# A mixture-of-experts layer in float32: the expert stage in quarter chunks, with its lists of tokens on chip

## The chip, the cores and the metric

The kernel runs on one core of a Trainium2 chip. A core has five engines that run side by side: TensorE (PE in the profile, with its weight loads as PEld), VectorE (DVE), ScalarE (ACT), GpSimd (POOL) and SyncE (SP), which here only issues DMAs. Engines wait for each other by semaphores. The metric is the time of one execution in microseconds, and less is better.

## What is computed

One decoder layer for 2048 tokens of width 1024: a mixer (gated linear attention and retention), and then a layer of 32 experts, each with a gate and up projection (1024 to 2048) and a down projection (1024 to 1024). Every token goes to its 4 best experts. The change concerns this second part:

```python
gu = lax.ragged_dot(xs, w_gu, group_sizes) + b_gu[sorted_e]
gate, up = jnp.split(gu, 2, axis=-1)
gate = jnp.minimum(gate, SWIGLU_LIMIT)
up = jnp.clip(up, -SWIGLU_LIMIT, SWIGLU_LIMIT)
act = (up + 1.0) * (gate * jax.nn.sigmoid(SWIGLU_ALPHA * gate))
out = lax.ragged_dot(act.astype(h.dtype), w_down, group_sizes) + b_down[sorted_e]
```

Run on the reference's inputs, the router gives 79 tiles of up to 128 tokens to the 32 experts: 3 2 1 1 4 3 1 4 3 1 2 1 4 1 2 2 2 3 1 1 2 2 5 2 3 1 5 2 8 2 1 4, in the order of the experts.

## The kernel before

Six phases run one after the other, with a barrier between them: modulation, projection, mixer, routing (`phase_routing`), experts (`phase_experts`) and the final norm.

At its end the routing phase works out a table of groups: an expert's tiles are cut into groups of up to four (`GT = 4`), so that its weights are loaded once for a group. The two experts with 5 tiles become 4 and 1, the one with 8 becomes 4 and 4: 35 groups for 32 experts, 47 places for them in the loops. Each engine runs the same loop over the groups and reads the table for itself (`field`, L1511: one load of a register from memory for each field). For places that hold no group it reads the number of tiles, finds 0 and goes on.

Within a group the weights come in six chunks of 1024 x 512 (`NCH`): four for gate and up (`NGU`), each of 256 gate and 256 up columns, and two for down. A chunk comes in two halves of 1 MB. Each half is loaded by SyncE in two DMAs with rows of 1 KB (L1568), rounded to a high part by ScalarE (`weights_hi`, L1634) and the rest is taken as a low part by VectorE (`weights_lo`, L1700). Four raw halves are held. A float32 product is then three products in the faster format: high by high, high by low, low by high (L111 to L113), so a tile takes 24 products of 128x512 for a chunk and 144 for its group. Two chunks of split weights are held, so ScalarE can write a half of chunk c + 2 once the last tile has gone past that half of chunk c.

Of a gate and up chunk VectorE adds the bias (L1716), clips (L1720, L1721), and multiplies (L1727, L1729) after ScalarE's sigmoid (L1674). Two transposes turn each result (`activations`, L1811), and it is split again (L1658, L1746). Of a down chunk VectorE multiplies by the token's share and g2 (`weigh`, L1755), and GpSimd adds the rows to `y_rows` in memory with an indirect DMA (L1617), which takes the rows' numbers from `rec_now`.

For the next group GpSimd loads the tokens' numbers (`rec_next`, L1581), gathers their rows (L1586), waits until they are there, and TensorE transposes them during the down chunks (`next_rows`, L1828). GpSimd does this after the last group's rows have landed in `y_rows` and after `rec_now` has come (L1605). ScalarE's first sigmoid of a group waits for the same landing (`y_added`), since `act_row` was a source of the last rows.

## Time and profile before

| | us |
|---|---|
| median of 3 runs (4604.93 to 4610.49) | 4606.93 |
| the profiled execution | 4608.54 |
| its span, first to last instruction | 4606.9 |
| of it, first to last product of the experts | 1546.1 to 4527.3 |

Twelve groups have one tile, ten two, five three and eight four. The profile's page lists the busy time of the engines, their groups of instructions and DMAs. The trace answers further questions: a timeline of single instructions (start, duration, and in brackets how long the engine had been idle and what ended that), busy times in chosen stretches, and groups of instructions by line. Times are from the start of the span.

### The profile page before, as it was taken

The page shows a single profiled execution, that of the slowest core. Times are in us where ns is not written, and L with a number is a line of the kernel's source. Part 1 is how long each engine was busy: PE and PEld are TensorE (multiplying, and loading weights), DVE is VectorE, ACT ScalarE, POOL GpSimd, SP SyncE. Part 2 cuts the span into 40 slices and gives each one's busy share as a digit, 9 for nine tenths or more (in the row PEclk, how much of TensorE's full clock was granted, in tenths as well). Part 3 has the DMA queues.
Part 4 walks back from the last instruction along what each step waited for, and adds up shares of the span by engine and source line. Part 5 has one row for each costly group of instructions (what it writes and reads, how often), then busy time and mean ns, then how long its engine had stood idle before and what let it go on. Part 6 is the DMA issues. An engine that isn't in the chain of part 4 may idle for free. (4 is left out here: it accounts for less than half of the span.)

```text
span 4606.9 us, 64078 instructions
## 1 busy us (share of the span) xinstructions
PE 4043.3 (88%) x18375; PEld 3256.1 (71%) x18376; DVE 2660.6 (58%) x4097; ACT 1566.9 (34%) x2223; POOL 779.6 (17%) x691
## 2 busy tenths in 40 slices
PE   7998996665898697998999999998999999999993
PEld 4886885554676575887877777876877777788772
DVE  4123123997566567556567667667657665655752
ACT  2213112555121234224244334444324333322422
POOL 1010011554122111011112011111111111110101
PEclk8998997787998799999999999999999999999996
DMA  6342333332221568356468477667648557644735
GB/s 230 110 163 97 110 132 117 107 108 102 104 105 73 165 193 275 120 148 209 133 191 250 144 223 228 200 205 256 208 117 265 164 182 203 203 126 116 236 96 168
DMA packets 557045, 758.35 MB, mean 165 GB/s; under 512 B 32602, under 2 KB 462980, under 8 KB 552372
## 3 DMA queue, kind: packets, MB, share of 16 engines
q1 hardware_dynamic: 494532, 587.16, 38.8%
q0 software_dynamic: 59856, 160.36, 13.4%
q10 hardware_dynamic: 2592, 9.96, 0.5%
q8 instruction: 40, 0.66, 0.1%
q14 instruction: 25, 0.20, 0.0%
HBM read 649.31 MB, written 108.07 MB: 164 GB/s over the span
## 5 line engine op out<-in xcount | busy, mean ns | idle before, releaser
L1700 DVE TENSOR_TENSOR exp_w_lo<-exp_w_raw,exp_w_hi 128x2048 fp32r<-128x2048 f32 x420 | 959.3, 2288 | 273.5 <-ACT exp_w_hi L1634 145.8
L111 PE MATMUL exp_bank_acc<-exp_w_hi,exp_x_hi 128*128 128x512 f32 x2528 | 1022.5, 404 | 87.4 <-DVE exp_w_lo L1700 65.9
L113 PE MATMUL exp_bank_acc<-exp_w_hi,exp_x_lo 128*128 128x512 f32 x2528 | 996.1, 394 | 0.0
L112 PE MATMUL exp_bank_acc<-exp_w_lo,exp_x_hi 128*128 128x512 f32 x2528 | 994.5, 393 | 0.0
L1634 ACT CAST exp_w_hi<-exp_w_raw 128x2048 fp32r<-128x2048 f32 x420 | 788.9, 1910 | 318.4 <-PE exp_bank_acc L113 255.1
L111 PEld LDWEIGHTS exp_bank_acc<-exp_w_hi,exp_x_hi 128*128 128x128 f32 x2528 | 480.5, 190 | 218.2 <-issue 85.3
L111 PE MATMUL exp_bank_acc<-exp_w_hi,exp_a_hi 128*128 128x512 f32 x1264 | 511.5, 405 | 61.2 <-DVE exp_a_lo L1746 43.5
L113 PEld LDWEIGHTS exp_bank_acc<-exp_w_hi,exp_x_lo 128*128 128x128 f32 x2528 | 480.0, 190 | 103.9
L112 PEld LDWEIGHTS exp_bank_acc<-exp_w_lo,exp_x_hi 128*128 128x128 f32 x2528 | 481.6, 191 | 92.4
L113 PE MATMUL exp_bank_acc<-exp_w_hi,exp_a_lo 128*128 128x512 f32 x1264 | 494.9, 392 | 0.0
L112 PE MATMUL exp_bank_acc<-exp_w_lo,exp_a_hi 128*128 128x512 f32 x1264 | 493.8, 391 | 0.0
L1617 POOL DMA_INDIRECT y_rows<-exp_weighted,exp_rec_now x100 | 162.8, 1628 | 1714.0 <-DVE exp_weighted L1755 1624.2
L1674 ACT ACTIVATE exp_act_row<-exp_gate_up 128x256 f32<-128x256 f32 x316 | 132.1, 418 | 799.4 <-DVE exp_gate_up L1720 694.2
L111 PE MATMUL pro_bank_acc<-pro_w_hi,pro_h_hi 128*128 128x512 f32 x896 | 356.1, 397 | 0.0
L113 PE MATMUL pro_bank_acc<-pro_w_hi,pro_h_lo 128*128 128x512 f32 x896 | 351.1, 392 | 0.0
L112 PE MATMUL pro_bank_acc<-pro_w_lo,pro_h_hi 128*128 128x512 f32 x896 | 351.0, 392 | 0.0
L1658 ACT CAST exp_a_hi<-exp_bank_ta 128x256 fp32r<-128x256 f32 x316 | 116.8, 370 | 625.5 <-PE exp_bank_ta L1811 625.5
L111 PEld LDWEIGHTS exp_bank_acc<-exp_w_hi,exp_a_hi 128*128 128x128 f32 x1264 | 238.1, 188 | 122.2 <-DVE exp_a_lo L1746 50.6
L1746 DVE TENSOR_TENSOR exp_a_lo<-exp_bank_ta,exp_a_hi 128x256 fp32r<-128x256 f32 x316 | 133.5, 422 | 278.0 <-ACT exp_a_hi L1658 263.6
L113 PEld LDWEIGHTS exp_bank_acc<-exp_w_hi,exp_a_lo 128*128 128x128 f32 x1264 | 237.7, 188 | 51.2
L112 PEld LDWEIGHTS exp_bank_acc<-exp_w_lo,exp_a_hi 128*128 128x128 f32 x1264 | 238.6, 189 | 43.7
L1716 DVE TENSOR_TENSOR exp_gate_up<-exp_bank_acc,exp_bias 128x512 f32<-128x512 f32 x316 | 215.8, 683 | 92.4 <-PE exp_bank_acc L113 90.9
(292 smaller groups left out, 4898.1 us busy)
## 6 DMA issues: line engine op xcount, KB each, us to landing
exp_w_raw<-in_w_gu SPq DMA_DIRECT2D x560, 512.0 KB
exp_w_raw<-in_w_down SPq DMA_DIRECT2D x280, 512.0 KB
exp_bias<-in_b_gu SPq DMA_DIRECT2D x35, 1024.0 KB, 8.4
early_w_raw<-in_w_in POOLq DMA_DIRECT2D x14, 2048.0 KB, 10.9
proj<-pro_stage SPq DMA_DIRECT2D x112, 256.0 KB
pro_w_ada<-in_w_ada POOLq DMA_DIRECT2D x64, 256.0 KB, 3.6
mix_proj<-proj SPq DMA_DIRECT2D x16, 768.0 KB, 4.6
mod_w_ada<-in_w_ada SPq DMA_DIRECT2D x8, 1024.0 KB, 15.1
```

The lines of the kernel that those rows point to most:

```text
L111: nc.tensor.matmul(out, act_hi, w_hi, start=first, stop=False)
L112: nc.tensor.matmul(out, act_hi, w_lo, start=False, stop=False)
L113: return nc.tensor.matmul(out, act_lo, w_hi, start=False, stop=last)
L1617: pool.indirect_dma_start(out=keep["y"][c - NGU], out_offset=bass.IndirectOffsetOnAxis(ap=rec_now[:, t, 0:1], axis=0), in_=weighted_at(c, ...
L1634: nc.scalar.copy(whi[:, c % 2, half * HK:(half + 1) * HK], raw[:, n % RAW]).then_inc(hi_done, 1)
L1658: nc.scalar.copy(ahi[:, t, 2 * c:2 * c + 2], ta[:]).then_inc(ahi_done, 1)
L1674: nc.scalar.activation(act_row[:, t], gu[:, t % 2, 0:H], ACT.Sigmoid, scale=SIG).then_inc(sg_done, 1)
L1700: nc.vector.tensor_tensor(wlo[:, c % 2, rows], raw[:, n % RAW], whi[:, c % 2, rows], ALU.subtract).then_inc(lo_done, 1)
L1716: nc.vector.tensor_tensor(gu[:, u].rearrange("p (a n) -> p a n", a=2), acc[:, bank(c, t)].rearrange("p (a n) -> p a n", a=2), bias[:, :, c ...
L1746: nc.vector.tensor_tensor(alo[:, t, 2 * c:2 * c + 2], ta[:], ahi[:, t, 2 * c:2 * c + 2], ALU.subtract).then_inc(alo_done, 1)
```

## The change

All of it is in the experts' phase, but for the table.

1. Weights in quarters: a chunk's 8 row blocks are loaded, rounded, subtracted and multiplied in 4 pieces of 512 KB (`PIECES = 4`), one DMA each with rows of 2 KB. Eight raw pieces are held, as many bytes as before. TensorE waits for each piece by itself in the first tile, and releases each by itself.
2. A chunk of gate and up is now 512 columns of gate (chunks 0 and 2) or of up (chunks 1 and 3). Bias, gate and product are done on 512 columns once per pair: one addition and one Silu for the gate; addition, clip and product for up. Four transposes per pair replace two per chunk. ScalarE now casts half of chunk 2 ahead of the gates of all tiles, and half of chunk 4 ahead of the second pair's gates.
3. Records on chip: all tokens' numbers and shares are loaded once (`rec`, 512 KB), and GpSimd copies a group's numbers with two small instructions. `rec_next`, `rec_now` and their waits are gone. The gather for the next group is issued ahead of all waits for landings, and its own landing isn't waited for on GpSimd.
4. Each landing is waited for by the instruction that overwrites the source. The last result of tile 0 goes through `gu[:, 1]`, all others through `act_row`.
5. Packed fields: tiles, next tiles, tiles before and place come in one word, with shifts. A count of groups replaces the reading of empty places.
6. Even last groups: where an expert's last group would have one tile, it takes one from the group before (5 tiles: 3 and 2).

```diff
             fin(nc.vector.tensor_scalar(table[:, 1:2], col[:, 6:7], float(GT), 0.0, ALU.min, ALU.max))
+
+            one = sel[:, 0:1]
+            fin(nc.vector.tensor_scalar(one, col[:, 6:7], 1.0, None, ALU.is_equal))
+            fin(nc.vector.scalar_tensor_tensor(out=one, in0=col[:, 5:6], scalar=0.0, in1=one, op0=ALU.is_gt, op1=ALU.mult))
+            fin(nc.vector.scalar_tensor_tensor(out=table[:, 1:2], in0=col[:, 6:7], scalar=GT + 1.0, in1=table[:, 1:2],
+                                               op0=ALU.is_equal, op1=ALU.subtract))
+            fin(nc.vector.tensor_tensor(table[:, 1:2], one, table[:, 1:2], ALU.subtract))
+            fin(nc.vector.tensor_tensor(col[:, 5:6], col[:, 5:6], one, ALU.subtract))
...
+    NCH, NGU = 6, 4
+    PIECES = 4
+    SK = KD // PIECES
+    RAW = 2 * PIECES
+    raw = k.sb("w_raw", [P, RAW, SK, N])
...
+    def place_in(w):
+        return (w >> 14).with_bounds(min_val=0, max_val=PLACES - GT)
...
-        def __init__(self, eng, g, T):
-            self.T = T
-            self.before = field(eng, g, BEFORE, NG * GT)
+        def __init__(self, eng, g):
+            self.word = load_word(eng, g)
+            self.T = tiles_in(self.word)
+            self.nT = (self.word >> 3) & 7
+            self.before = (self.word >> 6) & 255
...
                     expert = field(sp, g, EXPERT, E - 1)
-                    for n in range(2 * NCH):
-                        c, half = n // 2, n % 2
+                    for n in range(PIECES * NCH):
+                        c, j = n // PIECES, n % PIECES
                         if n == RAW:
 
-                            sp.wait_ge(act_done, G.before * NGU + 1)
-                            sp.dma_start(bias[:].rearrange("p a n -> p (a n)"),
-                                         gu_b[bass.ds(expert, 1), :].rearrange("o n -> (o n)").partition_broadcast(P)
+                            sp.wait_ge(act_done, G.before * 2 + 1)
+                            sp.dma_start(bias[:], gu_b[bass.ds(expert, 1), :].rearrange("o n -> (o n)").partition_broadcast(P)
                                          ).then_inc(bias_in, 16)
...
+                        sp.wait_ge(lo_done, G.pieces(n - RAW + 1))
+                        rows = slice(j * SK, (j + 1) * SK)
+                        w, col = (gu_w, column(c)) if c < NGU else (dn_w, (c - NGU) * N)
+                        sp.dma_start(raw[:, n % RAW], w[:, bass.ds(expert, 1), rows, col:col + N]).then_inc(raw_in[n % RAW], 16)
...
+            pool.wait_ge(rec_in, 16)
+            pool.sem_inc(wait_carrier, 1)
+            pool.wait_ge(word_set, 1)
+            for half in range(2):
+                pool.dma_start(keep["y"][half][S:S + 1, 0:NG + 1].bitcast(I32), word[:]).then_inc(y_out[half], 16)
+
+            def fetch_rows(g, T, place):
+
+                nc.gpsimd.tensor_copy(next_token[:], rec[:, bass.ds(place, GT), 0]).then_inc(next_set, 1)
+                pool.wait_ge(next_set, g + 1)
                 pool.sem_inc(wait_carrier, 1)
                 for t in range(GT):
...
-                pool.wait_ge(rows_in, (before + T) * 16)
-                pool.sem_inc(wait_carrier, 1)
...
-                    with pool.If(nT > 0):
+                with pool.If(count > g):
+                    G = Group(pool, g)
+                    place, nplace = place_in(G.word), place_in(load_word(pool, g + 1))
+                    with pool.If(G.nT > 0):
                         pool.wait_ge(tx_done, G.before + G.T + 1)
                         pool.sem_inc(wait_carrier, 1)
-                        fetch_rows(g + 1, nT, nplace, nbefore)
+                        fetch_rows(g + 1, G.nT, nplace)
+                    for half in range(2):
+                        pool.wait_ge(y_out[half], G.landed(0))
+                        pool.sem_inc(wait_carrier, 1)
+                    nc.gpsimd.tensor_copy(token[:], rec[:, bass.ds(place, GT), 0]).then_inc(token_set, 1)
+                    nc.gpsimd.tensor_copy(share[:], rec[:].bitcast(F32)[:, bass.ds(place, GT), 1]).then_inc(share_set, 1)
+                    pool.wait_ge(token_set, g + 1)
+                    pool.sem_inc(wait_carrier, 1)
                     for c in (NGU, NGU + 1):
                         for t in range(GT):
                             with pool.If(G.T > t):
-                                pool.wait_ge(weighted_done, G.down_tile(c, t))
+                                pool.wait_ge(read_done, G.chunk_tile(c, t))
                                 pool.sem_inc(wait_carrier, 1)
                                 pool.indirect_dma_start(
                                     out=keep["y"][c - NGU],
...
+                                    out_offset=bass.IndirectOffsetOnAxis(ap=token[:, t:t + 1], axis=0),
+                                    in_=weighted_at(c, t), in_offset=None, compute_op=ALU.add).then_inc(y_out[c - NGU], 16)
+            for half in range(2):
+                pool.wait_ge(y_out[half], total * 16 + 16)
...
             def weights_hi(g, n, freed):
 
...
+                act.wait_ge(raw_in[n % RAW], (g * (PIECES * NCH // RAW) + n // RAW + 1) * 16)
+                c, j = n // PIECES, n % PIECES
+                act.wait_ge(mm_piece[j], freed)
+                nc.scalar.copy(whi[:, c % 2, j * SK:(j + 1) * SK], raw[:, n % RAW]).then_inc(hi_done, 1)
 
...
+                    def gate(q, t):
+
+                        act.wait_ge(read_done, G.chunk_tile(2 * q, t))
+                        nc.scalar.activation(act_row[:, t], gu[:, t % 2], ACT.Silu, scale=SIG).then_inc(sg_done, 1)
 
                     def next_rows_hi(t):
                         with act.If(nT > t):
                             rows_hi(G.before + G.T, t)
 
...
+                    for n in range(PIECES, 2 * PIECES + PIECES // 2):
+                        weights_hi(g, n, G.chunks_before(n // PIECES - 1))
+                    for t in range(GT):
+                        with act.If(G.T > t):
+                            if t < 2:
+
+                                act.wait_ge(y_out[t], G.landed(0))
+                            gate(0, t)
+                    for n in range(2 * PIECES + PIECES // 2, 4 * PIECES):
+                        weights_hi(g, n, G.chunks_before(n // PIECES - 1))
+                    for t in range(GT):
+                        with act.If(G.T > t):
+                            activations_hi(0, t)
+                    for n in range(4 * PIECES, 4 * PIECES + PIECES // 2):
+                        weights_hi(g, n, G.chunks_before(3))
+                    for t in range(GT):
+                        with act.If(G.T > t):
+                            gate(1, t)
+                    for n in range(4 * PIECES + PIECES // 2, 5 * PIECES + PIECES // 2):
+                        weights_hi(g, n, G.chunks_before(n // PIECES - 1))
+                    activations_hi(1, 0)
                     next_rows_hi(0)
-                    weights_hi(g, 2 * NCH - 1, G.chunks_before(NGU))
+                    for n in range(5 * PIECES + PIECES // 2, 6 * PIECES):
+                        weights_hi(g, n, G.chunks_before(NGU))
                     for t in range(1, GT):
                         with act.If(G.T > t):
-                            activations_hi(NGU - 1, t)
+                            activations_hi(1, t)
...
+            def gate_bias(G, g, q, t):
+
+                c = 2 * q
+                if q == 0 and t == 0:
                     dve.wait_ge(bias_in, (g + 1) * 16)
-                u = t % 2
-                dve.wait_ge(act_done, G.gu_tile(c, t) - 1)
+                if q == 0 and t == 1:
+                    dve.wait_ge(y_out[1], G.landed(0))
+                if q == 0 and t < 2:
+                    dve.wait_ge(act_done, G.before * 2 + 1)
+                elif t < 2:
+                    dve.wait_ge(act_done, G.before * 2 + G.T + 1)
+                else:
+                    dve.wait_ge(sg_done, G.pair_tile(q, t - 2) - 1)
                 dve.wait_ge(mm_done, G.chunk_tile(c, t))
-                nc.vector.tensor_tensor(gu[:, u].rearrange("p (a n) -> p a n", a=2),
-                                        acc[:, bank(c, t)].rearrange("p (a n) -> p a n", a=2),
-                                        bias[:, :, c * H:(c + 1) * H], ALU.add).then_inc(read_done, 1)
+                nc.vector.tensor_tensor(gu[:, t % 2], acc[:, bank(c, t)], bias[:, column(c):column(c) + N],
+                                        ALU.add).then_inc(read_done, 1)
+
+            def up_times_gate(G, q, t):
+
+                c, u = 2 * q + 1, t % 2
+                dve.wait_ge(mm_done, G.chunk_tile(c, t))
+                if t < 2:
+                    dve.wait_ge(sg_done, G.before * 2 + G.T * (q + 1))
+                else:
+                    dve.wait_ge(act_done, G.pair_tile(q, t - 2))
+                nc.vector.scalar_tensor_tensor(out=gu[:, u], in0=acc[:, bank(c, t)], scalar=1.0,
+                                               in1=bias[:, column(c):column(c) + N], op0=ALU.add,
+                                               op1=ALU.add).then_inc(read_done, 1)
                 dve.wait_ge(read_done, G.chunk_tile(c, t))
...
+                nc.vector.tensor_scalar(gu[:, u], gu[:, u], LIMIT + 1.0, 1.0 - LIMIT, ALU.min, ALU.max).then_inc(clip_step, 1)
+                dve.wait_ge(clip_step, G.pair_tile(q, t) - 1)
+                nc.vector.scalar_tensor_tensor(out=act_row[:, t], in0=act_row[:, t], scalar=float(MOST_GATE),
+                                               in1=gu[:, u], op0=ALU.min, op1=ALU.mult).then_inc(act_done, 1)
...
+                        if c == NGU and t == 0:
+                            dve.wait_ge(share_set, G.g + 1)
+                        if c == NGU + 1 and t == 0:
+                            dve.wait_ge(y_out[1], G.landed(0))
+                        if c == NGU + 1 and t == 1:
+                            dve.wait_ge(y_out[0], G.landed(G.T))
...
+                        for n in range(PIECES):
+                            weights_lo(g, PIECES * (c + 1) + n)
                         for t in range(GT):
                             with dve.If(G.T > t):
...
+                                if c == 2:
+                                    activations_lo(0, t)
+                                if c % 2 == 0:
+                                    gate_bias(G, g, c // 2, t)
+                                else:
+                                    up_times_gate(G, c // 2, t)
+                    activations_lo(1, 0)
+                    for n in range(5 * PIECES, 5 * PIECES + PIECES // 2):
+                        weights_lo(g, n)
                     next_rows_lo(0)
-                    weights_lo(g, 2 * NCH - 1)
-                    dve.wait_ge(rec_now_in, (g + 1) * 16)
-                    dve.sem_inc(wait_carrier, 1)
+                    for n in range(5 * PIECES + PIECES // 2, 6 * PIECES):
+                        weights_lo(g, n)
...
-                                    if s == HK:
-                                        mm.then_inc(mm_half, 1)
+                                    if s and s % SK == 0:
+                                        mm.then_inc(mm_piece[s // SK - 1], 1)
                                         if t == 0:
-                                            pe.wait_ge(lo_done, G.halves(2 * c + 2))
+                                            pe.wait_ge(lo_done, G.pieces(PIECES * c + s // SK + 1))
+                                    if c == 2 and s == KD - 2:
+                                        activations(G, 0, t)
+                                    if c == NGU - 1 and t == 1 and s == KD // 2:
+                                        activations(G, 1, 0)
                                     if c == NGU and t > 0 and s == 0:
...
+                                        activations(G, 1, t)
+                                    if c == NGU and t == 0:
+                                        if s == 0:
+                                            pe.wait_ge(alo_done, G.before * 2 + G.T + 1)
+                                        if s == KD // 2:
                                             with pe.If(G.T < 2):
-                                                activations(G, NGU - 1, t)
+                                                activations(G, 1, t)
                                             next_rows(0)
-                                        pe.wait_ge(alo_done, G.gu_tile(NGU - 1, t))
+                                    if c == NGU and s == KD // 2:
+                                        pe.wait_ge(alo_done, G.pair_tile(1, t))
```

## Rows read from the trace of the kernel before

**Rows 1.** the page: busy us of each engine, share of the span, instructions

```profile
PE 4043.3 (88%) x18375; PEld 3256.1 (71%) x18376; DVE 2660.6 (58%) x4097; ACT 1566.9 (34%) x2223; POOL 779.6 (17%) x691
```

**Rows 2.** stretches: three of ten one-tile groups; the sum is of all ten

```profile
1770.70:1834.60 63.90, 45.41 (x184) 35.05 (x184) 43.43 (x46) 27.59 (x27) 12.28 (x8) 0.89 0.87 275
...
2378.70:2424.70 46.00, 38.22 (x169) 29.11 (x169) 37.95 (x42) 27.28 (x24) 7.18 (x6) 1.00 0.84 263
2498.60:2551.20 52.60, 40.89 (x185) 30.50 (x185) 41.68 (x45) 27.61 (x27) 13.24 (x9) 1.00 0.95 291
...
sum 511.50, PE 400.85 PEld 301.52 DVE 399.95 ACT 272.80 POOL 98.20; mean PE 40.09 PEld 30.15 DVE 39.99 ACT 27.28 POOL 9.82
```

**Rows 3.** stretches: one expert's groups of four and one tile; three tiles; two tiles

```profile
3307.20:3445.00 137.80, 136.07 (x616) 111.69 (x616) 72.26 (x120) 38.19 (x50) 16.84 (x11) 1.00 0.44 121
3445.00:3490.90 45.90, 38.24 (x168) 29.08 (x168) 38.11 (x42) 27.39 (x25) 8.24 (x6) 1.00 0.85 262
...
2274.50:2378.70 104.20, 102.46 (x464) 83.97 (x464) 60.55 (x93) 32.43 (x39) 11.60 (x9) 1.00 0.53 151
3490.90:3563.40 72.50, 70.58 (x328) 57.90 (x329) 54.03 (x72) 31.52 (x35) 10.45 (x9) 1.00 0.82 257
```

**Rows 4.** timeline of VectorE over one chunk of a one-tile group

```profile
2389.61 2.29 DVE L1700 TENSOR_TENSOR exp_w_lo<-exp_w_raw,exp_w_hi 128x2048 fp32r<-128x2048 f32 x1 [0.28 <-issue]
...
2392.62 0.68 DVE L1716 TENSOR_TENSOR exp_gate_up<-exp_bank_acc,exp_bias 128x512 f32<-128x512 f32 x1
...
2393.74 2.29 DVE L1700 TENSOR_TENSOR exp_w_lo<-exp_w_raw,exp_w_hi 128x2048 fp32r<-128x2048 f32 x1
...
2397.09 2.29 DVE L1700 TENSOR_TENSOR exp_w_lo<-exp_w_raw,exp_w_hi 128x2048 fp32r<-128x2048 f32 x1 [0.27 <-issue]
```

**Rows 5.** timeline of VectorE: where that group begins; two subtractions in a row

```profile
2382.91 2.29 DVE L1700 TENSOR_TENSOR exp_w_lo<-exp_w_raw,exp_w_hi 128x2048 fp32r<-128x2048 f32 x1 [3.54 <-issue]
...
2422.08 4.48 DVE L1700 TENSOR_TENSOR exp_w_lo<-exp_w_raw,exp_w_hi 128x2048 fp32r<-128x2048 f32 x2
```

**Rows 6.** timeline of TensorE: after transposes; five products in a row; two stalls

```profile
1570.42 0.48 PE L111 MATMUL exp_bank_acc<-exp_w_hi,exp_x_hi 128*128 128x512 f32 x1
1570.74 0.40 PE L112 MATMUL exp_bank_acc<-exp_w_lo,exp_x_hi 128*128 128x512 f32 x1
...
2382.95 0.39 PE L111 MATMUL exp_bank_acc<-exp_w_hi,exp_x_hi 128*128 128x512 f32 x1
...
2384.08 0.39 PE L113 MATMUL exp_bank_acc<-exp_w_hi,exp_x_lo 128*128 128x512 f32 x1
...
2346.54 1.04 PE L1803 MATMUL exp_bank_tx<-keep_const,exp_rows 128*128 128x128 f32 x8
2349.12 0.50 PE L111 MATMUL exp_bank_acc<-exp_w_hi,exp_a_hi 128*128 128x512 f32 x1 [1.54 <-DVE exp_a_lo L1746]
...
2396.09 0.50 PE L111 MATMUL exp_bank_acc<-exp_w_hi,exp_x_hi 128*128 128x512 f32 x1 [0.93 <-DVE exp_w_lo L1700]
```

**Rows 7.** groups of instructions: busy us, mean ns | idle before, releaser

```profile
L1700 DVE TENSOR_TENSOR exp_w_lo<-exp_w_raw,exp_w_hi 128x2048 fp32r<-128x2048 f32 x420 | 959.3, 2288 | 273.5 <-ACT exp_w_hi L1634 145.8 <-issue 118.8 <-DVE exp_weighted L1755 8.2
...
L1755 DVE SCALAR_TENSOR_TENSOR exp_weighted<-exp_bank_acc,exp_rec_now,exp_g 128x512 f32<-128x512 f32 x100 | 74.9, 749 | 245.9 <-PE exp_bank_acc L113 245.9
...
L1328 DVE TENSOR_TENSOR rou_h<-rou_h,rou_sh 128x1024 f32<-128x1024 f32 x16 | 19.6, 1225 | 0.6
...
L404 ACT ACTIVATE pro_squares<-early_x 128x1024 bf16<-128x1024 f32 x16 | 17.0, 1060 | 5.7 <-DMA early_x<-in_x 5.6
```

**Rows 8.** instructions of single lines: table loads, last accumulation, GpSimd's loop (min/median/max ns)

```profile
L1512 POOLq TENSOR_LOAD <-exp_table x223: 282/287/501, 1518.7 to 4547.1; - x112
...
L1617 POOL DMA_INDIRECT y_rows<-exp_weighted,exp_rec_now x100: 1541/1562/3575, 1628.7 to 4529.0; - x100
...
L1595 POOLq COMPARE_BRANCH  x47: 40/45/53, 1660.1 to 4547.9; - x47
```

**Rows 9.** a stretch in which SyncE loads rows of 2 KB (w_ada)

```profile
3.00:20.00 17.00, 10.88 (x20) 4.80 (x21) 4.41 (x13) 0.00 (x0) 0.80 (x2) 1.00 1.03 384
```

270 lines of the change are left out of this document (109 added, 161 removed).

## Prediction

> **What bounds it now.** The page first: TensorE is busy for 88% of the span, VectorE for 58% [rows 1]. Those are averages, and the chain of waits at the page's end only follows the final norm, so I read the stretches group by group. In groups of two, three and four tiles TensorE is busy all but 2 us (70.58 of 72.5, 102.46 of 104.2, 136.07 of 137.8) [rows 3]. In the ten one-tile groups of [rows 2] (the two that follow a group of four of their own expert are set apart) it is busy for 400.85 of 511.5 us. One, of 46.0 us, is typical; with four tiles next it is 52.6; the worst, right behind another one-tile group, takes 63.9. So TensorE bounds the large groups and something else the small ones. The instruction counts give the followers: 144 products and 8 transposes, and 8 for each next tile (160, 168 or 184; two, three and five of the ten).
>
> The timeline of VectorE shows what. Over one chunk of a one-tile group it goes from one subtraction (2389.61) to the same one of the next chunk (2397.09), 7.48 us, with next to no gap [rows 4]: 2 x 2.20 for weights (two in a row last 4.48, so the second starts 2.19 after the first [rows 5]), the rest for bias, clip, products and a split. TensorE needs 24 products for it. Five take 2384.08 - 2382.95 = 1.13 us, so one takes 0.226 and a chunk 5.44. It waits for `exp_w_lo`, here 0.93 us by the trace and 1.3 us from start to start, since an earlier product's tail is counted as busy [rows 6].
>
> **One-tile groups, the term that carries the sum.** VectorE's work per group. Weights: before, 12 subtractions at 2.20 from start to start. A 128x1024 one lasts 1.225 where 128x2048 lasts 2.288 [rows 7]. Back to back they overlap by 0.09, so 24 cost 24 x 1.135 = 27.2 against 26.4: 0.8 us more. The rest of four chunks was 4 x (7.48 - 4.40) = 12.3. Now it is two pairs, each gate bias 0.70, up (addition 0.77, clip about 0.45, product 0.77) 2.0, and split 0.65, some 3.35 and 0.5 for registers: 7.7. At the group's start VectorE stands for 3.54 us while it reads its fields [rows 5]. One load instead of three leaves 1.5 to 2: I take 1.7. Together: 0.8 - 4.6 - 1.8 = -5.6 us.
>
> The Trainium skill speaks against the quarters. VectorE: DVE Perf Modes, section on the TRN2 errata, has a fixed cost for each instruction on SBUF, (N+151)/0.96 ns, and advises large tiles. Its 1.224 us is the trace's 1.225; without the overlap that the trace shows, 24 would cost 2.1 us more than I take, 21 us over ten groups.
>
> What the end of a group depends on is TensorE, so I lay the new order out by hand, from its first product at 0, for two tiles next. VectorE subtracts pieces 4 to 7 by 6.9 (chunk 1 starts at 5.44 and wants a piece every 1.36: no stall), adds the gate bias by 7.6, pieces 8 to 11 by 12.3, up by 14.4. TensorE turns that at 15.0, inside chunk 2. Pieces 12 to 15 by 19.1, split and second gate 20.6, pieces 16 to 19 by 25.3, up 27.4. Here is the one long stall: TensorE has come to the middle of chunk 4 at 24.9 and waits until 27.5, turns it, turns next rows (8 transposes in 1.04 at most [rows 6]; I take 0.9), waits 0.6 for the split, and goes on at 29.5. Chunk 5 runs from 32.2 to 38.6. So 38.6 for two tiles next, 37.6 for one, 39.7 for three and 42.1 for four, where VectorE's split of rows comes between. ScalarE at 1.06 us for each piece [rows 7] stays ahead. A hand schedule leaves out waits: I take 39.5, 40.5, 42 and 44.5. Behind a one-tile group VectorE is late by some 3 us, and the bias comes late too (its DMA goes out after piece 7 of the next group rather than half 3): 48 and 45 for the two such. The ten: 2 x 39.5 + 2 x 40.5 + 45 + 3 x 44.5 + 42 (its follower has now three tiles) + 48 = 428.5. **Gain 83.** The bare schedule gives 406 (105). The floor is TensorE's busy 400.85.
>
> The waits of GpSimd go: it no longer loads records, and issues the gather some 20 us earlier. ScalarE's first gate waits only for the landing of half 0, issued a whole chunk before. The 63.9 us group holds most of this: 16 of the 83.
>
> **Even last groups.** Two experts with 5 tiles. Before, 137.8 + 45.9 = 183.7; now a group of three and one of two, 104.2 + 72.5 = 176.7 as they are [rows 3], 174.5 with the edits below. **Gain 2 x 9.2 = 18.4.**
>
> **Two tiles and more.** Removed: the stall in the middle of chunk 4, where TensorE waited for the split of tile 0 (1.54 shown, about 1.7 from start to start) [rows 6], since that result is now turned in chunk 3. The first product after transposes starts 0.32 before the next rather than 0.23 [rows 6]: 0.09, twice less per tile. Fewer loads at the group's edge, 0.3. Added, with no row that shows it: ScalarE holds all gates of the second pair until it has cast pieces 16 and 17, which need the last tile of chunk 2. `gu` has two buffers, so the gate bias of tile 2 waits for the gate of tile 0. Queued behind it on VectorE are pieces 16 to 19 and the up of tile 0, which TensorE wants at 8.2 us into chunk 3. By hand that comes at 7.6 for two tiles, 9.4 for three, 10.8 for four: no stall, 1.3 and 2.7. In chunk 4 the split of tile 1 stands behind pieces 20 to 23: 0 to 0.8, I take 0.75. Per group: 1.7 for two tiles (ten), 0.5 for three (five), -0.8 for four (six). **Gain 15.** The added waits are 44 us in all (12 x 0.75 + 7 x 2.05 + 6 x 3.45, with the groups of the edit above), so the bounds are 59 without them and -29 with twice as much.
>
> **Edges.** Last accumulation issued at 4529.0, GpSimd's loop ends at 4547.9 [rows 8]. Between lie its landing and 12 empty places, about 1.17 us each. One load (0.287) and its register work go from each: **gain 8**, 5 to 12. Start: `rec` (512 KB) before the first gather, the word, two small DMAs, in place of one record load: loss 2, bounds 0 to 8. Routing: seven small VectorE steps of 0.2: loss 1.4.
>
> **The sum**, on the profiled execution of 4608.5: 83 + 18.4 + 15 + 8 - 2 - 1.4 = 121, so 4487.5. The median stands 1.6 below that execution: **4486 us**, 2.6% less.
>
> **Rivals.** (a) *DMA takes VectorE's place.* For: in one-tile groups the DMA engines are busy 0.84 to 0.95 of the time [rows 2]. Against: they move 263 to 291 GB/s there in rows of 1 KB, about 310 for a full share, and 384 where SyncE loads rows of 2 KB [rows 9], as all weights now come. The ten groups' 140 MB (some 274 GB/s over 511.5 us) take 379 us at 370 GB/s, under 428, but 451 at 311. Were the larger rows worth nothing and the queues 0.95 full, they would take 475: 46 less gained, 4532.
>
> The Trainium skill, DMA: Bandwidth & Descriptors, section Bandwidth, advises DMAs of 1 MiB and more; these stay at 512 KB, and by the rule nothing would be gained from the larger rows. Rows 9 show 384 with DMAs of 1 MB.
>
> (b) *The gathered gates and waits cost more in large groups*, twice my estimate, since VectorE's order puts whatever is late ahead of pieces that others need: 44 less gained, 4530.
>
> (c) *Slower.* The same mechanism, stronger: ScalarE is in order, and stands at pieces 8 and 9 until the last tile of chunk 0, with all first gates behind it, and again at 16 and 17. If VectorE then falls behind by more than its slack, which is a chunk of one tile, 5.44 us, for each of the two pairs, every group of three or four (13 after the change) loses 2 x 5.4 us and more: 13 x 11 = 143 more than I take. That outweighs the 121 of gain: 4629. It decides from 9.3 us per group. Against: in a group of four VectorE is busy 72 of 138 us [rows 3], so it catches up.
>
> (d) *The schedule without my surcharge and without added waits*: 22 + 44 more, 4420.
>
> **Chances.** Forecast (4455 to 4515) 0.58; (a) 0.14; (b) 0.12; (d) 0.09; (c) 0.07. Range 4436 to 4550: it takes in (a) and (b) with some 20 us beyond, and leaves out (c) and the better half of (d). Under 0.2% is about what a measurement can't tell from no change. Faster by more: 0.92; within: 0.01; slower: 0.07.
>
> **What would show it.** Right: one-tile groups of 39 to 45 us, VectorE back to back in them, the worst near 48; `exp_rows` gathers in the first third of a group; the wait of TensorE for `exp_a_lo` gone in large groups and a wait for `exp_act_row` of 1 to 3 us in chunk 3 of those with three and four tiles; DMA share under 0.95 at over 300 GB/s; some 8 us less between the last product and the final norm. Wrong: ScalarE waiting for `exp_w_raw` in most one-tile groups (a), TensorE idle over 5 us in large groups (b, c), or one-tile groups still near 46.

## The result, and the profile after

The changed kernel takes 4440.72 us (median of 4 runs, 4436.95 to 4445.28), the kernel before 4608.71 us beside it. The ratio is 0.9636 (95% interval 0.9619 to 0.9653), and the time lies 45 us under the 4486 forecast. The profiled execution has a span of 4443.7 us where before it was 4606.9.

I split both spans at the first product of each group. All in us; the rows are rounded one by one:

| part of the span | before | after | gain | forecast |
|---|---|---|---|---|
| ten one-tile groups | 511.5 | 424.1 | 87.4 | 83 |
| two experts with five tiles | 369.8 | 347.9 | 21.9 | 18.4 |
| ten other groups of two | 730.7 | 698.5 | 32.2 | 17 |
| five other groups of three | 524.6 | 520.0 | 4.6 | 2.5 |
| six groups of four | 844.8 | 840.2 | 4.6 | -4.8 |
| ahead of the first product | 1546.1 | 1548.2 | -2.1 | -3.4 |
| behind the last product | 79.6 | 64.9 | 14.7 | 8 |
| span | 4606.9 | 4443.7 | 163.2 | 120.7 |

The busy times, from the page of the changed kernel (for [rows 1]):

```profile
PE 3998.1 (90%) x18375; PEld 3255.1 (73%) x18376; DVE 2431.6 (55%) x3422; ACT 1573.4 (35%) x2327; POOL 749.7 (17%) x728
```

TensorE issues the same 18375 instructions; that it is busy for 45 us less goes with the stalls, whose first part counts as the tail of the product ahead, and with some 12 us less at half clock (see the part on the clock below). VectorE lost 675 instructions and 229 us.

The one-tile groups of the changed kernel, to be held against [rows 2] (columns: stretch, its length, busy us of PE, PEld, DVE, ACT and POOL, granted clock, share of the DMA engines, GB/s):

```profile
1761.90:1811.50 49.60, 39.79 (x184) 30.48 (x184) 40.27 (x44) 28.65 (x35) 11.76 (x9) 1.00 1.00 353
...
2344.80:2383.10 38.30, 36.13 (x169) 29.18 (x167) 34.97 (x39) 27.70 (x32) 7.23 (x7) 1.00 0.92 308
2452.00:2498.20 46.20, 40.02 (x186) 32.01 (x184) 39.43 (x43) 27.73 (x34) 9.02 (x9) 0.96 0.96 323
...
sum 424.00, PE 378.56 PEld 302.05 DVE 371.20 ACT 276.11 POOL 78.68; mean PE 37.86 PEld 30.20 DVE 37.12 ACT 27.61 POOL 7.87
```

The typical one fell from 46.0 to 38.3, the one with four tiles next from 52.6 to 46.2, the worst from 63.9 to 49.6. The last has a full DMA share. The larger groups, for [rows 3]: an expert's three and two tiles, three tiles, two tiles behind a one-tile group, four tiles:

```profile
3210.40:3314.60 104.20, 103.18 (x474) 84.97 (x473) 52.74 (x64) 33.12 (x40) 12.96 (x12) 1.00 0.56 163
3314.60:3384.20 69.60, 69.28 (x321) 57.17 (x320) 45.13 (x52) 30.88 (x36) 8.83 (x9) 1.00 0.69 213
2241.50:2344.80 103.30, 102.28 (x466) 84.13 (x465) 51.56 (x62) 32.27 (x38) 11.08 (x10) 1.00 0.52 152
2383.10:2452.00 68.90, 68.54 (x312) 56.49 (x313) 46.01 (x52) 30.52 (x35) 11.62 (x8) 1.00 0.80 262
2498.20:2636.40 138.20, 135.96 (x617) 112.02 (x618) 59.77 (x76) 37.41 (x45) 15.09 (x12) 1.00 0.44 132
```

Groups of two are now TensorE and nothing else (68.54 of 68.9); in a group of four 2.2 us are still idle.

The best single view is TensorE's own waits over the experts' part (what for: us in total, times, longest). Before:

```profile
PE exp_bank_acc L111 <- DVE exp_w_lo L1700: 82.7, 98, 3.3
PE exp_bank_acc L111 <- DVE exp_a_lo L1746: 43.5, 29, 2.4
PE exp_bank_acc L111 <- issue: 19.3, 27, 2.5
PE exp_bank_tx L1803 <- DVE exp_x_lo L1706: 13.0, 11, 2.0
PE exp_bank_tx L1803 <- DMA exp_rows<-h_rows,exp_rec_next: 9.6, 6, 3.5
PE exp_bank_ta L1811 <- DVE exp_act_row L1729: 4.7, 3, 2.5
```

And after:

```profile
PE exp_bank_ta L1884 <- DVE exp_act_row L1797: 37.7, 25, 3.9
PE exp_bank_acc L112 <- DVE exp_w_lo L1757: 18.4, 16, 1.9
PE exp_bank_acc L112 <- DVE exp_a_lo L1815: 9.1, 32, 0.4
PE exp_bank_tx L1876 <- DVE exp_x_lo L1763: 6.9, 6, 2.0
PE exp_bank_acc L112 <- issue: 1.1, 2, 0.8
```

Register work and gathered rows are no longer waited for to speak of. The waits for the low parts of weights and activations (`exp_w_lo`, `exp_a_lo`) fell from 126.2 us to 27.5. One wait grew from 4.7 to 37.7, that for the activations before they are turned (`exp_act_row`).

### The profile page after: what moved, and what is told of

Same layout as the page of the kernel before. It is cut to its first block and busy times, and to the rows that moved or that the text cites. A ratio compares the mean times of both kernels' runs of the same rounds, so it can differ in the third digit from the quotient of the medians.

```text
span 4443.7 us, 64529 instructions
## 1 busy us (share of the span) xinstructions
PE 3998.1 (90%) x18375; PEld 3255.1 (73%) x18376; DVE 2431.6 (55%) x3422; ACT 1573.4 (35%) x2327; POOL 749.7 (17%) x728
## 5 line engine op out<-in xcount | busy, mean ns | idle before, releaser
L1664 ACT CAST exp_w_hi<-exp_w_raw 128x1024 fp32r<-128x1024 f32 x840 | 860.7, 1051 | 949.3 <-PE exp_bank_acc L114 834.5
L1757 DVE TENSOR_TENSOR exp_w_lo<-exp_w_raw,exp_w_hi 128x1024 fp32r<-128x1024 f32 x840 | 978.0, 1217 | 64.5 <-ACT exp_w_hi L1664 59.6
L112 PE MATMUL exp_bank_acc<-exp_w_hi,exp_x_hi 128*128 128x512 f32 x2528 | 999.8, 395 | 15.0 <-DVE exp_w_lo L1757 12.9
L1646 POOL DMA_INDIRECT y_rows<-exp_act_row,exp_token x123 | 195.6, 1590 | 2147.1 <-DVE exp_act_row L1827 2100.5
L1791 DVE SCALAR_TENSOR_TENSOR exp_gate_up<-exp_bank_acc,exp_bias 128x512 f32<-128x512 f32 x158 | 108.9, 689 | 320.4 <-PE exp_bank_acc L114 320.0
L1827 DVE SCALAR_TENSOR_TENSOR exp_act_row<-exp_bank_acc,exp_share,exp_g 128x512 f32<-128x512 f32 x123 | 92.0, 748 | 331.1 <-PE exp_bank_acc L114 322.7
L1780 DVE TENSOR_TENSOR exp_gate_up<-exp_bank_acc,exp_bias 128x512 f32<-128x512 f32 x158 | 108.4, 686 | 263.8 <-PE exp_bank_acc L114 117.3
L1688 ACT CAST exp_a_hi<-exp_bank_ta 128x512 fp32r<-128x512 f32 x158 | 92.4, 585 | 452.7 <-PE exp_bank_ta L1884 452.7
```

The lines of the kernel that those rows point to most:

```text
L112: nc.tensor.matmul(out, act_hi, w_hi, start=first, stop=False)
L1646: pool.indirect_dma_start(out=keep["y"][c - NGU], out_offset=bass.IndirectOffsetOnAxis(ap=token[:, t:t + 1], axis=0), in_=weighted_at(c, t ...
L1664: nc.scalar.copy(whi[:, c % 2, j * SK:(j + 1) * SK], raw[:, n % RAW]).then_inc(hi_done, 1)
L1688: nc.scalar.copy(ahi[:, t, 4 * q:4 * q + 4], ta[:]).then_inc(ahi_done, 1)
L1757: nc.vector.tensor_tensor(wlo[:, c % 2, rows], raw[:, n % RAW], whi[:, c % 2, rows], ALU.subtract).then_inc(lo_done, 1)
L1780: nc.vector.tensor_tensor(gu[:, t % 2], acc[:, bank(c, t)], bias[:, column(c):column(c) + N], ALU.add).then_inc(read_done, 1)
```

## The experiments

The theory of the prediction: VectorE's work and the order of its queue set the one-tile groups, TensorE the others, and the added waits cost a little in groups of three and four. The chief rival: DMA, either the weights' rate or the landings that GpSimd waits for. Unless it says otherwise, a run is the changed kernel with one edit. Each run was timed beside the kernel before on its chip (its medians there 4604.8 to 4607.5, here 4608.7), so two ratios differ surely where their intervals are apart. Durations of groups are cut as in the table above.

**1. The gate of the second pair, earlier.**

```diff
                         with act.If(G.T > t):
+                            if t > 0:
+                                gate(1, t - 1)
                             activations_hi(0, t)
...
                         with act.If(G.T > t):
-                            gate(1, t)
+                            with act.If(G.T < t + 2):
+                                gate(1, t)
```

> The changed kernel with one thing moved: ScalarE issues the second pair's gate of tile t - 1 between the casts of the first pair's activations of tiles t - 1 and t, and not after the casts of all tiles and half of chunk 4's weights; the gate of the last tile stays where it is. Theory of the queue order: the stalls of 1.1 us (three tiles) and 2.3 us (four tiles) in chunk 3, in which TensorE waits for the first pair's activations, come from a late gate, since the up products of tiles 0 and 1 free their accumulators only behind it. Then the stalls go in the 7 groups of three and the 6 groups of four tiles: 7 x 1.1 + 6 x 2.3 = 21.5 us at most, so about 4420 us, and one-tile groups stay within 0.5 us each. Rival: VectorE's own work sets those stalls, and the gates would have been on time. Then the large groups stay within 0.3 us each and the time is that of the changed kernel, 4441 us. Third: the early gates delay the casts of the activations, and the transposes of pair 0 wait for them: four-tile groups get longer by 1 us per cast behind a gate, 6 x 3 us, about 4459 us.

Measured: 4414.18 us, ratio 0.9585 (0.9572 to 0.9598), apart from the changed kernel's. Groups of three fell by 1.2 us each (728.5 to 720.0 for seven), groups of four by 3.1 (840.2 to 821.8 for six), one-tile groups by 4.1 in all, of which 2.7 in a single one (44.4 to 41.7). TensorE in a group of four, first the changed kernel and then this one (start, duration, idle before):

```profile
2573.45 0.39 PE L114 MATMUL exp_bank_acc<-exp_w_hi,exp_x_lo 128*128 128x512 f32 x1
2575.90 0.65 PE L1884 MATMUL exp_bank_ta<-keep_const,exp_act_row 128*128 128x128 f32 x4 [2.07 <-DVE exp_act_row L1797]
```

```profile
2559.08 0.40 PE L114 MATMUL exp_bank_acc<-exp_w_hi,exp_x_lo 128*128 128x512 f32 x1
2559.32 0.60 PE L1887 MATMUL exp_bank_ta<-keep_const,exp_act_row 128*128 128x128 f32 x4
```

The stall of 2.45 us from start to start is 0.24. The theory of the queue order holds, against VectorE's own work. In groups of four that is 2.2 of the 3.1 us; most of the rest is TensorE's granted clock, which in the changed kernel was at half for 22 products of these groups and here for none (see the part on the clock below). This version is faster than both kernels; of those that leave out no work only run 12 equals it.

**2. Without even last groups.**

```diff
-            one = sel[:, 0:1]
-            fin(nc.vector.tensor_scalar(one, col[:, 6:7], 1.0, None, ALU.is_equal))
...
-            fin(nc.vector.tensor_tensor(col[:, 5:6], col[:, 5:6], one, ALU.subtract))
```

> The changed kernel without the rule for even last groups: five tiles are again a group of four and a group of one. By the trace of the changed kernel a group of four tiles takes 139 to 140 us and one of one tile 43 us, two groups of three and two tiles 104.2 + 69.7 = 173.9 us. Theory of the sum (two experts, each 139.5 + 43 - 173.9 = 8.6 us): 17 us slower, about 4458 us. Rival: the group of one tile behind a large group finds its weights already there and costs only its TensorE work of 35 us, which the next group does not pay back: 0.6 us per expert, within 3 us of the changed kernel.

Measured: 4451.49 us, 0.9663 (0.9648 to 0.9678): 10.8 more by the medians, 6.7 by the spans, and the interval still touches that of the changed kernel. The groups say more: the two experts' pairs take 139.8 + 37.9 and 138.2 + 38.4 us where three and two tiles take 104.2 + 69.7 and 104.3 + 69.7, so 6.4 more in all, and the one-tile group ahead of one of them 45.6 rather than 41.1, since it has four tiles next. The result lies between my two cases and, by the intervals, is not surely apart from no change. A one-tile group behind a large one of its own expert costs 38, not the mean of 43 that I had put in.

**3. Halves of a chunk.**

```diff
-    PIECES = 4
+    PIECES = 2
```

> The changed kernel with PIECES = 2: each chunk comes in two pieces of 1 MB and no longer in four of 512 KB; everything else stays (rows of 2 KB, casts on 128x2048). Theory of the prediction: the size of the pieces sets how much of VectorE's and ScalarE's work lies ahead of the first product of a chunk that is late, since TensorE cannot begin with a piece before it is subtracted whole. One-tile groups: at each of 6 chunks the start comes later by one quarter, 1.1 us, as far as the chunk is late at all, which holds for 2 to 4 of the 6: 2 to 4 us for each of ten groups, 20 to 45 us in all, about 4475 us. Rival 1: the gain of the one-tile groups is VectorE's work that was taken away (fewer and larger instructions), and the pieces do nothing: within 10 us of the changed kernel, and rather faster, because half as many instructions save 0.1 us each where VectorE is bound. Rival 2: DMA sets the one-tile groups; pieces of twice the size are moved as fast, and each raw piece is freed later, so single groups behind one another get longer by 3 us or more each in the rows in which ScalarE waits for a raw piece. The Trainium skill (DMA: Bandwidth & Descriptors) asks for DMAs of 1 MiB and more; by it the larger pieces would come faster and these waits would shrink.

Measured: 4484.0 us, 0.9729 (0.9714 to 0.9744). One-tile groups +2.1 each (445.4 in all), two tiles +0.5, three +0.5, four +1.3. TensorE's waits:

```profile
PE exp_bank_acc L112 <- DVE exp_w_lo L1757: 42.3, 27, 4.2
PE exp_bank_ta L1884 <- DVE exp_act_row L1797: 29.5, 24, 3.2
PE exp_bank_acc L112 <- DVE exp_a_lo L1815: 18.7, 33, 0.6
```

`exp_w_lo` is at 42.3 where quarters have 18.4, and the split of the activations at 18.7 against 9.1. VectorE has half as many subtractions, and the kernel is slower, with TensorE waiting longer for the low parts: what counts is how much stands ahead of the first product. (The casts and the DMAs became larger too, so their shares are not told apart; and of the 8 us that the groups of four lost, some 3.6 are 18 more products at half clock.) By the Trainium skill (DMA: Bandwidth & Descriptors, section Bandwidth) the pieces of 1 MB would come faster; ScalarE waited 97.7 us for raw pieces here and 92.3 in the changed kernel, so no such gain shows.

**4. Rows of 1 KB.**

```diff
-                        sp.dma_start(raw[:, n % RAW], w[:, bass.ds(expert, 1), rows, col:col + N]).then_inc(raw_in[n % RAW], 16)
+                        for part in range(2):
+                            cols = slice(part * (N // 2), (part + 1) * (N // 2))
+                            sp.dma_start(raw[:, n % RAW, :, cols],
+                                         w[:, bass.ds(expert, 1), rows, col + cols.start:col + cols.stop]).then_inc(raw_in[n % RAW], 16)
```

> The changed kernel with each piece of weights loaded by two DMAs whose rows are 1 KB, as they were before the change, and not by one with rows of 2 KB; the bytes and their order stay. Theory of VectorE and queue order: large groups have cover, and the one-tile groups are bound by VectorE and TensorE, not by the loads: within 10 us of the changed kernel, 4441 to 4451 us. Rival, DMA sets the time of the one-tile groups (12.6 MB of weights in 38 to 50 us are 250 to 330 GB/s): the kernel before moved at most about 310 to 330 GB/s with rows of 1 KB, the changed one 370 to 384 GB/s. Then the ten one-tile groups get longer by 3 to 6 us each, 30 to 60 us in all, 4471 to 4501 us, and most in the groups behind another one-tile group.

(Each piece then comes as two DMAs of 256 KB; ScalarE's wait counts both.) Measured: 4446.66 us, 0.9654 (0.964 to 0.9669), not to be told from the changed kernel. The ten one-tile groups take 425.2 us. The DMA engines had a little more to do for the same bytes (in one such group a share of 0.97 at 299 GB/s, in the changed kernel 0.90 at 299), but the time did not follow. The larger rows, on which my case against rival (a) leaned, were worth next to nothing.

**5. The kernel before, with half of the subtractions.**

```diff
                 rows = slice(half * HK, (half + 1) * HK)
-                nc.vector.tensor_tensor(wlo[:, c % 2, rows], raw[:, n % RAW], whi[:, c % 2, rows],
+                rows = slice(half * HK, half * HK + HK // 2)
+                nc.vector.tensor_tensor(wlo[:, c % 2, rows], raw[:, n % RAW, 0:HK // 2], whi[:, c % 2, rows],
```

> The kernel before, in which VectorE subtracts only the first half of each half of the weights; the low part of the other half is left out (set to zero once ahead of the loop), while TensorE multiplies as before. A subtraction takes 1.22 us instead of 2.29, 12 per group: 13 us less of VectorE's work. Theory, VectorE's work sets the ten one-tile groups of the kernel before (VectorE busy for 399.95 of 511.5 us, TensorE for 400.85): they fall to 415 to 440 us in all, so some 80 us less than before, 4525 us, and the large groups move little. Rival, the waits for records and landings set them: the ten stay over 490 us, and the time is within 20 us of the kernel before. In between, what is left above 415 to 440 is the share of the waits and of DMA.

The other half of the low part is left out (zero), TensorE multiplies as before. Measured: 4537.48 us, 0.9849 (0.9833 to 0.9866), 70 less than the kernel before. But the ten one-tile groups fell only from 511.5 to 485.2, near the rival's 490; the rest came in the other groups, above all behind one-tile groups (two tiles: 73.9 to 70.1, 74.8 to 70.6). Why so little, TensorE's waits tell:

```profile
PE exp_bank_tx L1807 <- DMA exp_rows<-h_rows,exp_rec_next: 40.5, 9, 6.7
PE exp_bank_acc L111 <- DVE exp_w_lo L1704: 29.6, 47, 2.2
PE exp_bank_acc L111 <- DVE exp_a_lo L1750: 13.1, 23, 1.3
```

`exp_w_lo` fell from 82.7 to 29.6, and the gathered rows rose from 9.6 to 40.5. A second part is the clock: TensorE ran 75 products of the ten groups at half clock, where the kernel before ran 25, some 10 us of the missing gain. Still, the kernel before had two bounds in the same groups, one right behind the other: VectorE, and a gather whose first part was issued 20 to 32 us into the group. What made it late was above all the load of records. GpSimd's waits in the kernel before:

```profile
POOL exp_rec_next L1581 <- DMA exp_rec_now<-places: 137.3, 34, 5.5
POOL exp_rows L1586 <- DMA exp_rec_next<-places: 101.6, 33, 5.7
```

That is 7 us in each group. My theory named only the first bound.

**6. The changed kernel, with half of the subtractions.**

```diff
-                nc.vector.tensor_tensor(wlo[:, c % 2, rows], raw[:, n % RAW], whi[:, c % 2, rows],
+                rows = slice(j * SK, j * SK + SK // 2)
+                nc.vector.tensor_tensor(wlo[:, c % 2, rows], raw[:, n % RAW, 0:SK // 2], whi[:, c % 2, rows],
```

> The changed kernel with the same cut: VectorE subtracts only the first half of each piece, 128x512 in place of 128x1024, some 0.66 us in place of 1.22; the low part of the other half of the weights is left out (zero). 24 x 0.55 = 13 us less of VectorE's work per group. Theory, VectorE's work still sets the one-tile groups: they fall from 424 to some 375 to 390 us in all (TensorE is busy for 35 to 40 us in each), and the one right behind another falls from 49.6 and 44.4 to near 42; the time is 4441 - 40 = 4400 us, a little less with the stalls of large groups. Rival, DMA sets the groups that have four tiles next (41 to 50 us) and those behind another one-tile group: these six stay above 42 us, only the four at 38 lose 1 to 2 us each, and the time is within 12 us of 4441, in spite of a third less work on VectorE.

The same work is left out. Measured: 4386.42 us, 0.9525 (0.9509 to 0.9541). The ten fell from 424.1 to 398.2, where TensorE was busy for 378.6 in the changed kernel. Where one or two tiles come next they take 35.3 and 36.2, which is TensorE alone (but 42.0 behind another one-tile group). The four with four next keep 42.2 to 47.4, 2 to 4 us less than in the changed kernel, with VectorE busy for only 28:

```profile
2042.00:2084.90 42.90, 38.43 (x185) 30.86 (x183) 28.09 (x45) 27.54 (x34) 8.25 (x9) 1.00 0.94 334
1754.50:1802.00 47.50, 41.15 (x186) 32.98 (x185) 28.25 (x45) 28.62 (x35) 8.26 (x10) 0.93 1.04 375
```

So VectorE sets the groups at 38 us. In the six above 40 something else takes over after 2 to 4 us. The loads are the likely part of it, since ScalarE still waits there, but no run took them away, so this is argued and not shown; the turns and splits of up to four next tiles are in those groups as well. In the worst group of the changed kernel ScalarE waits for raw pieces (first line the total in that group, then single casts):

```profile
ACT exp_w_hi L1664 <- DMA exp_w_raw<-in_w_gu: 14.2, 8, 4.4
```

```profile
1764.86 1.05 ACT L1664 CAST exp_w_hi<-exp_w_raw 128x1024 fp32r<-128x1024 f32 x1 [1.95 <-DMA exp_w_raw<-in_w_gu]
1770.30 1.05 ACT L1664 CAST exp_w_hi<-exp_w_raw 128x1024 fp32r<-128x1024 f32 x1 [4.39 <-DMA exp_w_raw<-in_w_gu]
```

**7. A later gather, and 8. one as late as before.**

```diff
                         pool.wait_ge(tx_done, G.before + G.T + 1)
                         pool.sem_inc(wait_carrier, 1)
+                        pool.wait_ge(read_done, G.chunk_tile(2, 0))
+                        pool.sem_inc(wait_carrier, 1)
                         fetch_rows(g + 1, G.nT, nplace)
```

(This is run 8. Run 7 has these lines without the two new ones, but behind the waits for `y_out`, and a wait for `rows_in` behind them.)

> The changed kernel with the gather of the next group's rows issued where the kernel before issued it, behind GpSimd's wait for the landing of the group's previous results, and with its own landing waited for on GpSimd before the group's numbers are copied. Theory of the prediction: rows are wanted only in chunk 4, and the early gather does nothing for the time but in the group behind another one-tile group, within 5 us of 4441. Rival 1: the early gather carries part of the gain, since a late one delays the turns of the next rows: 2 to 4 us for each one-tile group, 20 to 40 us slower. Rival 2: the early gather is harmful, since its 512 KB per tile stand ahead of the weights of chunks 2 and 3 on the same engines, just where ScalarE waits for a raw piece (1.4 and 3.0 us in the one-tile group with four tiles next): then the late one is faster by 1 to 3 us in each of the six one-tile groups of over 40 us, 6 to 18 us in all.

> The changed kernel with the gather of the next group's rows issued as late as the kernel before issued it: GpSimd waits first until VectorE has added the gate bias of chunk 2 of tile 0, which is 21 us into a one-tile group (before: 20 to 31 us; changed kernel: 5 to 13; the run late_gather: 9 to 20, at no cost). Theory, the gather was a second bound right behind VectorE's work: in the kernel before with VectorE's subtractions halved, TensorE waited up to 3.5 us for the gathered rows in the middle of chunk 4. Rows are wanted some 27 us into the group and land 4.4 to 11.6 us behind their issue: with one tile next 0 to 1 us, with two 2 to 3, with three 4, with four 6 us for each group. 2 x 0.5 + 3 x 2.5 + 4 + 4 x 6 = 36 us, about 4477 us; large groups unchanged. Rival: VectorE alone sets one-tile groups and TensorE would have stood anyway at that place: within 8 us of 4441.

Measured, run 7: 4442.78 us, 0.9645 (0.9629 to 0.9661), no difference; the gathers went out 9 to 21 us into the one-tile groups, the first of each at 9 to 16. Run 8: 4486.16 us, 0.9736 (0.972 to 0.9752), 45.4 more. All of it is in the ten one-tile groups (424.1 to 469.3: +1.8 and 3.2 with one tile next, 1.6 to 4.8 with two, 5.4 with three, 3.6 to 7.8 with four); the groups of two stay within 0.1 us, those of three but for the first too, and those of four take 0.5 less on the mean. Some 5 of the 45 us are again the clock (41 products at half clock in the ten groups, not 15). TensorE's wait for the rows:

```profile
PE exp_bank_tx L1878 <- DMA exp_rows<-h_rows,exp_next_token: 63.5, 10, 10.4
```

Together the two runs draw the line: with its first part issued by 16 us into a one-tile group the gather costs nothing, from 21 to 25 us (the last part by 29) it costs 2 to 8. Earlier than that it is worth nothing more.

**9. Fields read singly, five words, and 10. as before, three words.** Run 10:

```diff
-        def __init__(self, eng, g):
-            self.word = load_word(eng, g)
-            self.T = tiles_in(self.word)
-            self.nT = (self.word >> 3) & 7
-            self.before = (self.word >> 6) & 255
+        def __init__(self, eng, g, T):
+            self.T = T
+            self.before = field(eng, g, BEFORE, NG * GT)
...
-                with pe.If(count > g):
-                    G = Group(pe, g)
-                    nT = G.nT
+                T = field(pe, g, TILES, GT)
+                with pe.If(T > 0):
+                    G = Group(pe, g, T)
+                    nT = field(pe, g + 1, TILES, GT)
```

(Run 9 keeps the word as well and reads tiles twice.)

> The changed kernel with the fields read one by one again: each engine loads tiles, next tiles and tiles before as three words at the start of a group, and every engine asks for the tiles of each of the 12 empty places at the end. Theory of the prediction: VectorE stands at a group's start for 1.3 us more, which only one-tile groups feel, 1 to 1.5 us in each of ten, and GpSimd's way through the empty places costs 8 us more behind the last product: 18 to 23 us slower, 4461 us. The changed kernel won 14.7 us behind the last product and not 8: if the empty places are all of it, this kernel gives back 14 to 15 there, 4468 us. Rival: TensorE reads fields too, and its reads at the edge are on the path of every group, 0.6 us each in 35 groups: 20 us more than the above, over 4475.

> The changed kernel with the fields read exactly as the kernel before reads them: three words per group and engine on TensorE, VectorE and ScalarE (tiles, tiles before, next tiles), one after the other at the group's start, no packed word, and the tiles of each empty place at the end. The run called fields read five words, the packed one among them, and TensorE stood for 2.0 us at the edge of every group, large ones too: its sequencer runs ahead of the array by about two reads, and each read takes 0.82 us from one to the next. Theory of the run-ahead: with two reads less, 0.4 us are left of the 2.0 on TensorE (25 large groups: 9 us), and two reads more than the changed kernel on VectorE at 0.7 us in each of ten one-tile groups (14 us); 7 behind the last product and 3 ahead of the first: 33 us slower than the changed kernel, 4474 us. Rival 1: reads of TensorE in any number cost their full 0.82 us each: 1.6 us in each of 35 groups, 57 us and 10 for the edges, 4508 us. Rival 2, my first estimate (18 to 23 us, 4461 us), in which only one-tile groups feel the reads.

Measured, run 9: 4549.51 us, 0.9871 (0.9855 to 0.9888): 109 more where I expected 20. TensorE stands at the edge of most groups, here between two groups:

```profile
1729.78 0.39 PE L114 MATMUL exp_bank_acc<-exp_w_hi,exp_a_lo 128*128 128x512 f32 x1
1731.77 0.49 PE L112 MATMUL exp_bank_acc<-exp_w_hi,exp_x_hi 128*128 128x512 f32 x1 [1.60 <-issue]
```

and in all for

```profile
PE exp_bank_acc L112 <- issue: 57.5, 29, 3.6
```

At this edge the sequencer's own records show it done with the old group at 1726.73, 3.05 us before the last product of that group starts. Its five reads follow one another at 0.67 to 0.89 us, and with the register work around them it needs 4.9 us until the new group's first instructions: 1.9 more than it was ahead, which is about the stall (1.99 from start to start, less the 0.23 of a product).

Run 10: 4486.14 us, 0.9736 (0.9719 to 0.9752), 45.4 more, against 33 from the run-ahead and 67 from the full price. With two reads fewer TensorE's `issue` waits are 6.4 us. Groups of two lose 0.4 each, of three 0.5, one-tile groups 10.7 in all, groups of four 2.2 each (my 0.4 was too low there), and 7.7 go behind the last product. The run-ahead holds: reads are free as long as TensorE's sequencer is ahead of the array by more than they take, and beyond that they cost. But of the 2.2 us in a group of four 1.3 are the clock: 61 products of these six groups ran at half clock, where it was 22 in the changed kernel. In run 9 it was 150 products in all against 49, some 20 of its 109 us.

**11. Eighths of a chunk.**

```diff
-    PIECES = 4
+    PIECES = 8
```

> The changed kernel with PIECES = 8: pieces of 256 KB, casts and subtractions on 128x512. With halves every one-tile group became 2.1 us longer, two- and three-tile groups 0.5, four-tile groups 1.3. Theory, two effects against each other: a finer piece lets TensorE start up to 0.55 us earlier where it waits (gain 1 us per one-tile group, 0.2 in the others), but 48 subtractions at some 0.60 us from start to start are 28.8 us of VectorE's time where 24 at 1.135 are 27.2: 1.6 us lost in each one-tile group. Sum +0.6 x 10 - 0.2 x 25 = 1 us: 4441 within 10 us, so quarters are near the best size. Rival: the start of a chunk is what counts, and the series of halves and quarters goes on: half of the 43 us that halves cost, gained once more, 4420 us. Third: ScalarE or the loads fall behind with twice as many instructions and DMAs: over 4460 us.

Measured: 4455.38 us, 0.967 (0.9654 to 0.9687), 14.7 more. One-tile groups took 2.4 us less in all, not 6 more; the larger ones lost: two tiles 0.4 each, three 0.6, four 1.0. The price is where I had not looked: in a group of four the stall in chunk 3 grew from 2.45 to 2.9 us from start to start, and the wait for a split in chunk 4 from 0.56 to 0.84. A chunk's subtractions stand in both queues, now eight instead of four. Quarters are the best of the three sizes.

**12. Run 1, with one subtraction moved.**

```diff
-                    activations_lo(1, 0)
-                    for n in range(5 * PIECES, 5 * PIECES + PIECES // 2):
+                    weights_lo(g, 5 * PIECES)
+                    activations_lo(1, 0)
+                    for n in range(5 * PIECES + 1, 5 * PIECES + PIECES // 2):
```

> The run gates2 (4414 us) with one more thing moved: VectorE subtracts piece 20 ahead of the split of the second pair's activations of tile 0, and not behind it. In one-tile groups VectorE stands idle for 1.37 to 1.4 us ahead of that split, until TensorE has turned the activations and ScalarE has cast them; a subtraction from start to start is 1.14 us. Theory, VectorE's time sets the middle of a one-tile group: 1.0 to 1.1 us less in each of ten, 4414 - 10 = 4404 us; large groups unchanged within 0.2 us. Rival: the split comes 1.1 us minus the idle time later for TensorE, which waits for exp_a_lo in the middle of chunk 4 already (0.4 us in the trace), and what VectorE wins is DMA's or the next rows' to lose: within 4 us of 4414, one-tile groups unchanged or 0.3 us longer.

Measured: 4413.16 us, 0.9584 (0.9571 to 0.9597), the same as run 1. One-tile groups with one or two tiles next did fall by about 1 us (38.0 to 36.8, 38.1 to 37.1, 38.4 to 37.6, 37.7 to 36.5), of the four with four tiles next two fell by 0.2 and 1.3 and two rose by 0.4 and 1.1, and groups of four gave 3 us back. That fits run 6: VectorE sets the first kind, more than VectorE the second. Most of the 3 us of the groups of four stand in two of them. One began with 7 products at half clock, 1.4 us. In the last one the split now stands behind the moved subtraction, and TensorE waits for it in the middle of chunk 4, where in run 1 it did not:

```profile
4299.66 0.39 PE L114 MATMUL exp_bank_acc<-exp_w_hi,exp_a_lo 128*128 128x512 f32 x1
4301.20 0.50 PE L112 MATMUL exp_bank_acc<-exp_w_hi,exp_a_hi 128*128 128x512 f32 x1 [1.15 <-DVE exp_a_lo L1818]
```

## Why the prediction came out as it did

**What bounds the kernel**: right in place, incomplete in cause. TensorE bounds large groups and something else the small ones. "VectorE" was half of it: run 5 shows the gather right behind it as a second bound. The prediction took the gather's 20 us as slack given away ("issues the gather some 20 us earlier") and priced it only in the 63.9 us group. Run 8 prices it at 45 us, over half of the 87.4 that the one-tile groups won. The sum of these groups still came out, because the new order was laid out from TensorE's side with rows that were simply there in time: the layout had the early gather built in without saying so. That is luck of the method, not foresight.

**One-tile groups**, 428.5 forecast and 424.1 measured. The single groups held too: 38.0, 37.7 with one tile next (39.5 forecast), 38.4 twice (40.5), 41.1 (42), 45.1, 46.1, 45.3 (44.5), 49.6 (48) and 44.4 (45). The bare layout gave 406, though, and the 22 us that I put on top came from no row; that they fit so closely is luck in part. The overlap of subtractions stands. VectorE, four subtractions in a row, then the pair's addition, clip and product, and the split:

```profile
2364.77 4.62 DVE L1757 TENSOR_TENSOR exp_w_lo<-exp_w_raw,exp_w_hi 128x1024 fp32r<-128x1024 f32 x4
2369.31 0.68 DVE L1791 SCALAR_TENSOR_TENSOR exp_gate_up<-exp_bank_acc,exp_bias 128x512 f32<-128x512 f32 x1
2370.03 0.43 DVE L1795 TENSOR_SCALAR exp_gate_up<-exp_gate_up 128x512 f32<-128x512 f32 x1
2370.49 0.69 DVE L1797 SCALAR_TENSOR_TENSOR exp_act_row<-exp_act_row,exp_gate_up 128x512 f32<-128x512 f32 x1
...
2372.55 0.69 DVE L1815 TENSOR_TENSOR exp_a_lo<-exp_bank_ta,exp_a_hi 128x512 fp32r<-128x512 f32 x1 [1.37 <-ACT exp_a_hi L1688]
```

4.62 us for four is 3 x 1.135 + 1.22, the number I took. By the fixed cost for each instruction that the Trainium skill gives (VectorE: DVE Perf Modes, the section on the TRN2 errata), taken without overlap, the ten groups would have been 21 us longer, an estimate; the trace decides for the overlap. What follows from it, larger tiles, was tested by run 3 and had the wrong sign here (the page asks for 512 elements and more, which all these sizes have): with fewer, larger pieces the kernel took 43 us more, and TensorE waited 24 us more for `exp_w_lo`. The long stall stood where the hand schedule had it, before the turn of pair 1, but with 1.7 us from start to start and not 2.6:

```profile
2369.53 0.39 PE L114 MATMUL exp_bank_acc<-exp_w_hi,exp_a_lo 128*128 128x512 f32 x1
2371.24 0.66 PE L1884 MATMUL exp_bank_ta<-keep_const,exp_act_row 128*128 128x128 f32 x4 [1.32 <-DVE exp_act_row L1797]
2371.80 1.09 PE L1876 MATMUL exp_bank_tx<-keep_const,exp_rows 128*128 128x128 f32 x8
2373.29 0.50 PE L112 MATMUL exp_bank_acc<-exp_w_hi,exp_a_hi 128*128 128x512 f32 x1 [0.40 <-DVE exp_a_lo L1815]
```

**Even last groups**: 21.9 in the table against 18.4, but run 2 leaves 11 at most to the edit itself. The rest is the shorter one-tile groups, which the experts with five tiles would have had as well, and 2.2 us of clock: the second expert's group of four began at half clock and took 140.4 us, and the forecast was worked out from the first alone (137.8). The step compared the new pair with the old 45.9 us group and not with the 38 us that the other edits make of it.

**Two tiles and more**: the term that was mis-sized, 41.4 us against 15. The forecast stalls of chunk 3 are there as worked out: 1.24 us from start to start for three tiles and 2.45 for four, less the 0.23 of a product 1.0 (1.3 forecast) and 2.2 (2.7). The wait in chunk 4 is 0.5 for two tiles and 0.3 for more, not 0.75. So the added waits cost 12 x 0.5 + 13 x 0.3 + 7 x 1.0 + 6 x 2.2 = 30 us and not 44. The larger miss is on the other side: a one-tile group hands its lag to the group behind it. Four of the five groups of two behind a one-tile group won 4.5 to 5.2 us each, where I had 1.7 for all; the other five won 1.8 to 3.0. Run 5 shows whose lag it is: with half the subtractions three of these four groups fell by 3.3 to 4.2 us in the kernel before (73.9 to 70.1), the fourth by 1.7, and the groups of two behind larger ones by 1. In three of the four 1.2 to 1.6 us of the loss were products at half clock, which came back as well. The step failed because it costed a group by its own stalls in chunks 3 and 4, and left those in its first chunks to its predecessor, where nobody counted them.

**Edges**: 14.7 won behind the last product, not 8. GpSimd's walk through the empty places ends 8.5 us behind the last product rather than 20.6. An empty place fell from 1.17 to 0.59 us, 7 for the twelve, which is the term as forecast (8); 4 to 5 us more came since the landing of the last accumulations is now waited for behind that walk and no longer ahead of it, and 2.5 since the drain behind the loop lasts 2.3 us and no longer 4.8. Run 10 gave 7.7 us of this part back.

**Registers**, spread over three terms: 1.8 for VectorE in ten groups, 0.3 at the edge of 25, 8 for the empty places, 33 in all. Run 10 gave back 45 by the medians, as much as the gather or the quarters, and 41 by the spans: 10.7 in one-tile groups, where I had 18, 21 in the larger ones, where I had 8 (13 of it in groups of four, 8 of these the clock), 7.7 at the end.

**The clock**, a term that the prediction put at nothing without a word. In stretches TensorE's granted clock is at 0.50, the lower of its two levels (1.2 and not 2.4 GHz), and products follow one another at 0.43 us and not 0.226. In the changed kernel, behind the stall in chunk 3 of a group of four (the last line: the clock is 0.50, the DMA share 0.53):

```profile
3922.10 0.65 PE L1884 MATMUL exp_bank_ta<-keep_const,exp_act_row 128*128 128x128 f32 x4 [2.07 <-DVE exp_act_row L1797]
3923.55 0.63 PE L112 MATMUL exp_bank_acc<-exp_w_hi,exp_x_hi 128*128 128x512 f32 x1
3923.98 0.63 PE L113 MATMUL exp_bank_acc<-exp_w_lo,exp_x_hi 128*128 128x512 f32 x1
3923.00:3926.10 3.10, 3.10 (x8) 2.33 (x8) 0.00 (x0) 0.00 (x0) 0.00 (x0) 0.50 0.53 205
```

Such stretches lie inside one-tile groups, at the start of the group behind one, at the start of the first group, and now and then behind that stall (in the changed kernel once in six). Counted by the distance of products, 107 ran at half clock in the kernel before, 49 in the changed one and 20 in run 1: at 0.2 us each some 21, 10 and 4 us. So about 12 of the 163 us won are clock that came back as the waits went: 2 in the ten one-tile groups, 4 in groups of two, 4 in the six groups of four, 2 in the experts with five tiles.

**Rivals.** (a) DMA takes VectorE's place: ScalarE's waits for raw pieces rose from 10.8 to 92.3 us:

```profile
ACT exp_w_hi L1634 <- DMA exp_w_raw<-in_w_gu: 10.8, 8, 1.9
ACT exp_w_hi L1664 <- DMA exp_w_raw<-in_w_gu: 77.0, 49, 4.9
ACT exp_w_hi L1664 <- DMA exp_w_raw<-in_w_down: 15.3, 38, 2.4
```

The sign that the prediction set for (a) came true: ScalarE waits in all ten one-tile groups, 3.9 to 15.2 us in each, and the DMA share there is 0.88 to 1.00. But the sign was a poor one: run 6 took the groups at 38 us down to TensorE's own time with such waits still in them. In the six over 40 us the loads may cost some us, and not the 46 that I had set, and rows of 1 KB make no difference. (b) and (c) are out: no large group lost more than the stalls above. (d), no surcharge and no added waits (4420), is the nearest by time, but not by cause: the one-tile groups took 424 and not 406, and the added waits are there. Run 1 is what (d) had in mind for the large groups.

Undone one by one in the changed kernel, by the medians: early gather 45, packed word 45, quarters rather than halves 43, even groups 11 and rows of 2 KB 6 (both within error), early gates on top -27. The first five sum to 151 of the 168 gained. They need not add up, since each was undone with the others in place. VectorE's merged gate work was not undone alone, so its own share stays open.

## What to carry to other kernels

A stretch with one late engine can have a second bound hidden right behind it. Take the first away for a look (half the work, as in run 5), and read what the critical engine waits for then; run 5, which removed only one of the two, won 26 us in the one-tile groups of the 72 to 97 that its theory promised. Cost a small group with what it hands to its successor, count the reads at a loop's edge against how far the sequencer of the critical engine runs ahead, and look at the granted clock wherever the critical engine waits: a stall can cost more than its length. The size of a piece has its optimum where what it puts ahead of the first product and what its instructions add in the queue balance; one run on either side tells whether one is near it.

## What the runs showed of the hardware

- Register reads on TensorE's sequencer (0.67 to 0.89 us from one to the next in run 9) are hidden while it is ahead of the array, by 3.05 us at the edge shown, and cost after that: with one word per group its `issue` waits are 1.1 us in all, with three 6.4 and with five 57.5.
- Rows of 1 KB in DMAs of 256 KB, rather than rows of 2 KB in DMAs of 512 KB, left the time of this kernel the same within error (4446.66 against 4440.72), though about 350 GB/s are moved in the group that waits most for its weights (353, and 346 with the smaller rows). The DMA share for 299 GB/s rose from 0.90 to 0.97.
- 128x1024 subtractions of VectorE follow one another at 1.135 us while one lasts 1.22; with the overlap of 0.08 to 0.09 four pieces take 4.62 us, 3% more than two of twice the size (4.48 [rows 5]).
- After waits TensorE's granted clock was at 0.50 for stretches of some 3 us (0.50 from 3923.00 to 3926.10), and a product then took 0.43 us instead of 0.226. The stall of 2.04 to 2.07 us in chunk 3 was followed by such a stretch in one of the six groups of four.
